# A two-layer hybrid state-space, attention and expert kernel: readout products reordered, mask added by VectorE in pieces, next layer's modulation products moved

## The chip, the core and the metric

The kernel runs on one core of one Trainium2 chip. The time is that of the device, in microseconds (us), from start to end of one execution, lower being better. A core has TensorE (matrix products; PE in the profile, PEld for its weight loads), VectorE (DVE), ScalarE (ACT), GpSimd (POOL) and SyncE (SP), each with a queue of its own that it works off in order. TensorE writes to PSUM, which has eight banks here: four take turns for products (`tile_ps`), two take transposes (`turn_ps`), two attention outputs (`out_ps`).

## What is computed

Two layers over 256 context and 256 latent tokens of width 1024, all in float32. A layer normalises its input, scales and shifts it by vectors made from a condition (the modulation), projects it once, and runs three mixers on the result. Then come a gated merge, an output projection and a mixture of 16 experts, two per token. The parts that the change touches, cut from the reference:

```python
sh1, sc1, g1, sh2, sc2, g2 = jnp.split((cond_lat @ w_mod[layer] + b_mod[layer])[:, None, :], 6, axis=-1)
...
# state space mixer: states are scanned both ways, then read out
y_lat = (readout(st_f[:, n_ctx:], 0) + readout(st_b[:, :n_lat], 1) + dsk * u_lat.astype(f32))
...
# grouped attention: query and key heads are normalised and rotated first
qa_h = rmsnorm(heads(qa, GQA_HEADS), q_norm_g)
...
# neighbourhood attention: scores get a bias table, and columns out of the window are masked
s_loc = jnp.einsum('bqhd,bikhd->bhqik', q_row, kb).astype(jnp.float32) * scale + bias[None]
s_loc = jnp.where(col_mask[None, None, :, None, :], s_loc, -jnp.inf)
```

## The kernel before

The order of work is written out by hand for each engine. `tile_jobs()` lists the jobs in TensorE's order; a job's place in the list, modulo 4, is its PSUM bank, and it may start when the job four places ahead has been taken out by ScalarE or VectorE. Weights stream through a ring of six 1 MB slots that SyncE refills as TensorE releases them, in the order of `slot_steps()`.

**Readout loop.** The 32 groups of state channels are read out in eight quarters of four groups, q = 0 to 7, with a ninth round for the last. For each q:

- GpSimd makes the coefficients `cp` of q in six operations (L1640 to L1645) in one of two buffers; it may start when the products `y` of q - 2 are complete.
- TensorE makes the lag products `z` of q (16 matrix products of 64 to 16, 32 records in the trace) from `cp`.
- ScalarE copies `z` out, VectorE adds the other half and the skip term (`readout_rows`), and ScalarE then issues eight DMAs (L1045) that spread it into the matrix `tm` of q. VectorE brings the carried states in (`carry_in`).
- TensorE makes `y` and `yb` of q (20 products, 40 records) from `tm`, `cp` and the states. They wait for the DMAs of `tm` (`tm_in`). ScalarE copies `y`, VectorE adds `yb` (L1479).

In round q the kernel before runs `z` of q first and `y` of q - 1 behind it. In the same round TensorE runs one part of the head norm (`qk_ms`, q up to 4), the modulation row product `mr` of block 4 + q (eight products over two ring slots), a projection (`in_loop`: two in round 0, one in each of rounds 1 to 4), the modulation columns `mc`, which wait for ScalarE's copy of the row (`mrow`), and the rotation `rope` (q up to 4). `rope` waits for `qnorm_done`: ScalarE takes a root, VectorE a reciprocal (L1486), and one more operation (L1487) scales the head. The root stands behind the eight DMA issues in ScalarE's queue. The `y` copy does too.

**Attention.** Layer 0 has 32 pairs of head and 128-query block, layer 1 has 16; half of them are grouped attention, the second half neighbourhood attention. In round n TensorE makes the scores of pair n, the transposes of pair n - 3 and the outputs of pair n - 4. VectorE takes maxima (L1514), reciprocals (L1520) and copies transposes (L1524); ScalarE takes exponentials (L1073); GpSimd scales the probabilities (L1660). In rounds 0 to 3 ScalarE also issues the four DMAs of the bias table (L972), in round 4 those of `yt` (L1085). GpSimd adds the mask of far columns to the table in two operations of 128x2048 ahead of pair 12 in layer 0 and pair 6 in layer 1 (L1654), once all four DMAs have landed (`bias_in`). In layer 0 the modulation blocks 0 to 3 of layer 1 (`mr`, ScalarE's copy, `mc`) stand in rounds 3, 7, 11 and 15.

## Time and profile before

| what | value |
|---|---|
| median of 3 runs | 2008.54 us (2006.32 to 2015.71) |
| the profiled execution | 2010.74 us, of it span 2009.1 us |
| TensorE busy | 1714.0 us (85%), mean granted clock 0.923 |
| VectorE, ScalarE, GpSimd busy | 637.3, 409.3, 347.9 us |
| readout loop, layer 0 and layer 1 | 209.9 to 336.2 us, 1307.4 to 1437.7 us |
| attention, layer 0 and layer 1 | 336.2 to 463.3 us, 1437.7 to 1508.9 us |

The span is from the first to the last instruction. A share of busy time is a mean over stages with different limits, so each stage is read by itself. The clock is what TensorE was granted: 1.0 is 2.4 GHz and 0.5 is 1.2 GHz, and a stretch's value is the mean of its parts at either. In the timeline a row joins instructions of one line that follow each other; the brackets say how long the engine had been idle and what released it. "ACTq" rows are DMA issues, during which ScalarE starts nothing else.

### The profile page before, as it was taken

How to read it: one execution, taken by the hardware profiler on the slowest of the kernel's cores; microseconds unless marked ns; L12 is line 12 of the kernel's file. 1: busy time of each engine (PE TensorE's matmuls, PEld its weight loads, DVE VectorE, ACT ScalarE, POOL GpSimd, SP SyncE). 2: the span in 40 equal slices, each digit the busy share in tenths (PEclk: the TensorE clock that was granted, in tenths of full speed). 3: DMA queues.
4: the chain of work that ended last, by engine and by line, in shares of the span. 5: the costliest groups of instructions: out<-in, count | busy, mean ns of one | idle time of the engine just before them, and what ended most of it. 6: DMA issues, size and time to landing. Idle time of an engine off the chain costs nothing.

```text
span 2009.1 us, 25439 instructions
## 1 busy us (share of the span) xinstructions
PE 1714.0 (85%) x9646; PEld 1049.6 (52%) x9646; DVE 637.3 (32%) x1378; ACT 409.3 (20%) x842; POOL 347.9 (17%) x284
## 2 busy tenths in 40 slices
PE   4999987899999998499979588998879994797794
PEld 1467554454444443355545336755458883464452
DVE  2578642351110113111101367774351112110012
ACT  3111211452000003122212231121242002121122
POOL 0004353681000000100000100435480000000000
PEclk8999986899999999699999788998789997899896
DMA  8411356508412125599999422145703427999992
GB/s 315 149 59 63 122 204 165 164 19 293 168 63 105 67 80 208 210 377 357 384 395 397 145 80 69 43 163 200 166 19 126 168 84 324 341 390 398 399 375 79
DMA packets 104882, 398.33 MB, mean 198 GB/s; under 512 B 43056, under 2 KB 52272, under 8 KB 64336
## 3 DMA queue, kind: packets, MB, share of 16 engines
q1 hardware_dynamic: 46960, 327.01, 41.9%
q10 hardware_dynamic: 50720, 29.54, 6.2%
q0 software_dynamic: 7104, 40.37, 5.9%
q8 instruction: 73, 1.20, 0.2%
q14 instruction: 25, 0.20, 0.0%
HBM read 370.67 MB, written 38.80 MB: 204 GB/s over the span
## 4 chain that ended last, share of the span: by engine, by line
PE 60%; DMA 14%; POOL 7%; DVE 6%; issue 5%; SPq 3%; ACT 3%; ACTq 1%; POOLq 0%; DVEq 0%
PE tile_ps L534 53%; DMA arena<-sorted_in 5%; PE turn_ps L534 4%; SPq L481 3%; DMA ring<-in_wpack 3%; POOL arena L1660 2%; DMA vn<-in_wpack 2%; DMA arena<-in_wpack 2%; PE out_ps L534 1%; DMA sorted_in<-arena,rows 1%; POOL arena L1654 1%; PE turn_ps L749 1%; ACTq L1045 1%; DVE rstd L1316 1%; POOL arena L1645 1%
## 5 line engine op out<-in xcount | busy, mean ns | idle before, releaser
L534 PE MATMUL tile_ps<-h,ring 128*128 128x512 f32 (+1 forms) x1312 | 475.3, 517 | 10.7 <-ACT h L930 8.0
L534 PEld LDWEIGHTS tile_ps<-h,ring 128*128 128x128 f32 x1312 | 250.6, 193 | 221.1 <-issue 206.0
L534 PE MATMUL tile_ps<-arena 64*16 64x128 f32 (+4 forms) x2032 | 244.2, 359 | 37.2 <-POOL arena L1645 16.5
L534 PE MATMUL tile_ps<-arena,ring 128*128 128x512 f32 (+1 forms) x704 | 235.3, 486 | 2.7 <-issue 2.7
L534 PEld LDWEIGHTS tile_ps<-arena 128*64 128x64 f32 (+3 forms) x2032 | 170.9, 161 | 94.1 <-issue 51.3
L534 PEld LDWEIGHTS tile_ps<-arena,ring 128*128 128x128 f32 x704 | 133.6, 190 | 96.6 <-issue 87.6
L1660 POOL TENSOR_SCALAR arena<-arena,smx 128x512 f32<-128x512 f32 (+1 forms) x96 | 127.9, 1349 | 86.8 <-DVE smx L1520 86.4
L534 PE MATMUL tile_ps<-ring,arena 128*64 128x256 f32 (+1 forms) x624 | 101.5, 469 | 9.9 <-ACT arena L1131 7.2
L1684 POOL DMA_DIRECT2D arena<-sorted_in x40 | 20.4, 511 | 515.7 <-PE tile_ps L834 515.7
L1112 ACT ACTIVATE arena<-tile_ps 128x512 f32<-128x512 f32 (+1 forms) x56 | 27.5, 491 | 347.4 <-PE tile_ps L534 347.4
L1581 DVE TENSOR_TENSOR arena<-tile_ps,arena 64x256 f32<-64x256 f32 x40 | 16.7, 417 | 228.2 <-ACT arena L1128 228.2
L1548 DVE TENSOR_TENSOR arena<-tile_ps,arena 128x512 f32<-128x512 f32 (+1 forms) x32 | 17.9, 558 | 212.1 <-PE tile_ps L534 212.1
L1640 POOL TENSOR_TENSOR arena<-arena 128x640 f32<-128x640 f32 x16 | 22.0, 1375 | 360.1 <-PE tile_ps L534 359.9
L1620 POOL TENSOR_SCALAR h<-h,amuls,mods 128x256 f32<-128x256 f32 x12 | 12.1, 1014 | 404.1 <-DVE h L1320 356.9
L834 PE MATMUL tile_ps<-con,arena 64*128 64x64 f32 x336 | 35.1, 227 | 50.4 <-DMA arena<-sorted_in 50.4
L1574 DVE COPY arena<-tile_ps 128x512 f32<-128x512 f32 x42 | 29.1, 692 | 146.9 <-PE tile_ps L834 146.9
L1073 ACT ACTIVATE arena<-tile_ps,smx 128x512 f32<-128x512 f32 (+1 forms) x96 | 58.7, 616 | 77.9 <-DVE smx L1514 68.1
L534 PEld LDWEIGHTS tile_ps<-ring,arena 128*64 128x64 f32 x624 | 51.3, 143 | 43.5 <-issue 34.0
L749 PE MATMUL turn_ps<-con,arena 128*128 128x128 f32 x320 | 51.8, 291 | 25.8 <-POOL arena L1660 9.3
L534 PE MATMUL tile_ps<-ring,h 128*128 128x256 f32 (+1 forms) x384 | 72.7, 352 | 0.0
L534 PE MATMUL turn_ps<-kn,arena 128*64 128x256 f32 x240 | 59.4, 398 | 11.6 <-DMA vn<-in_wpack 9.8
L534 PEld LDWEIGHTS tile_ps<-ring,h 128*128 128x128 f32 x384 | 64.6, 195 | 7.1
(258 smaller groups left out, 2157.2 us busy)
## 6 DMA issues: line engine op xcount, KB each, us to landing
ring<-in_wpack SPq DMA_DIRECT2D x176, 1024.0 KB, 7.9
arena<-in_wpack SPq DMA_DIRECT2D x64, 1024.0 KB, 28.8
h<-in_wpack SPq DMA_DIRECT2D x20, 1024.0 KB, 27.9
qa<-in_wpack SPq DMA_DIRECT2D x12, 1024.0 KB, 14.4
qn<-in_wpack SPq DMA_DIRECT2D x12, 1024.0 KB, 16.6
kn<-in_wpack SPq DMA_DIRECT2D x12, 1024.0 KB, 18.6
vn<-in_wpack SPq DMA_DIRECT2D x12, 1024.0 KB, 21.0
arena<-sorted_in POOLq DMA_DIRECT2D x42, 256.0 KB, 7.6
```

The lines of the kernel that those rows point to most:

```text
L481: sp.dma_start(dst, src).then_inc(arrived, 16)
L534: return nc.tensor.matmul(out, lhsT, rhs, start=start, stop=stop)
L749: ins = nc.tensor.transpose(turn_ps[:, half, t * P:(t + 1) * P], probs[:, N % (LAG + 1), half, t * P:(t + 1) * P], c("ident"))
L834: ins = nc.tensor.transpose(rows_bank[:, k * BS:(k + 1) * BS], hrow[:, k * P:(k + 1) * P], c("ident")[0:BS, 0:BS])
L1045: act.dma_start(tm[j * GRP:(j + 1) * GRP, q % 2], zs[:, :, a:a + P]).then_inc(tm_in, 16)
L1073: A(probs[:, N % (LAG + 1), half, 0:nk], bank((l, "sc", n, half))[:, 0:nk], ACT.Exp, bias=smx[:, 0, at:at + 1], accum_out=smx[:, 1, at:at ...
L1112: free(job, A(sig[:, n % 2, c0:], bank(job)[:, c0:], ACT.Sigmoid))
L1316: link(dve.reciprocal(rstd[:, c0:], rstd[:, c0:]))
L1574: CP(hsT.rearrange("p k n -> p (k n)"), rows_bank).then_inc(hsT_done[l], 1)
L1640: link(TT(o0, pv[0], cv[0], ALU.mult))
L1660: pool.tensor_scalar(v, v, smx[:, 2, at:at + 1], None, ALU.mult).then_inc(prob_done, 1)
L1684: pool.dma_start(hrow, sorted_in[bass.ds(r * BS, BS)]).then_inc(hrow_in[l], 16)
```

## The change

Four edits, in both layers except the last.

- In each round of the readout loop `y` and `yb` of q - 1 now come ahead of `z` of q, on TensorE, ScalarE and VectorE alike. ScalarE's `y` copy so comes ahead of the eight DMA issues.
- The projections in the loop stand in rounds 0 (two), 1, 2, 4 and 5 instead of 0 (two), 1, 2, 3 and 4.
- The mask is added by VectorE in eight pieces of 128x512, two at the end of each of four rounds that end just ahead of neighbourhood attention: rounds 12 to 15 in layer 0, 4 to 7 in layer 1. VectorE waits for `bias_in` at the first of them, and for each piece before it goes on. GpSimd's two operations and the semaphore `bias_done` go.
- In layer 0, the products `mr` of block 0 of layer 1 stand ahead of the last `y`; its columns and block 1 stand between the loop and attention, and blocks 2 and 3 stand in rounds 1 and 2 of attention.

```diff
@@ -108,7 +108,7 @@
 BRANCHES = (1, 2, 0)
-EVERY = 4
+EARLY = {1: 2, 2: 3}
 
...
@@ -128,7 +128,7 @@
 
-    return fill[IN_LOOP:IN_LOOP + 2] if q == 0 else fill[IN_LOOP + 1 + q:IN_LOOP + 2 + q]
+    return [fill[IN_LOOP + n] for n, at in enumerate((0, 0, 1, 2, 4, 5)) if at == q]
 
...
@@ -204,18 +204,19 @@
         for q in range(NQ + 1):
+            names += [(l + 1, "mr", 0)] if q == NQ and l + 1 < LAYERS else []
+            names += [(l, "y", q - 1), (l, "yb", q - 1)] if q else []
             names += [(l, "z", q, 0), (l, "z", q, 1)] if q < NQ else []
-            names += [(l, "y", q - 1), (l, "yb", q - 1)] if q else []
             names += [(l, "qk_ms", q)] if q <= KW else []
             names += [(l, "mr", MOD1 + q)] if q < NQ else []
             names += in_loop(fill, q)
             names += [(l, "mc", MOD1 + q)] if q < NQ else []
             names += [(l, "rope", q)] if q <= KW else []
+        names += [(l + 1, "mc", 0)] + mod_jobs(l + 1, [1]) if l + 1 < LAYERS else []
         n_pairs = len(attention_pairs(l))
         for u in range(n_pairs + LAG + 1):
             names += [(l, "sc", u, 0), (l, "sc", u, 1)] if u < n_pairs else []
-            if l + 1 < LAYERS and u % EVERY == EVERY - 1 and u // EVERY < MOD1:
-                names += mod_jobs(l + 1, [u // EVERY])
+            names += mod_jobs(l + 1, [EARLY[u]]) if l + 1 < LAYERS and u in EARLY else []
         for kind, *at in mix_order():
...
@@ -675,18 +676,8 @@
                 for q in range(NQ + 1):
-                    if q < NQ:
-                        pe.wait_ge(cp_done, l * NQ + q + 1)
...
-                                             cp[d, r, at_q, lags].rearrange("p a b -> p (a b)"), r == 0, r == 1)
-                                    if (g, r) == (GQ - 1, 1):
-                                        full((l, "z", q, n), ins)
+                    if q == NQ and l + 1 < LAYERS:
+                        modulation(l + 1, 0, l)
                     if q:
...
@@ -706,6 +697,18 @@
                         full(bwd, b)
+                    if q < NQ:
+                        pe.wait_ge(cp_done, l * NQ + q + 1)
+                        for n in range(2):
+                            wait_bank(pe, (l, "z", q, n))
...
+                                        full((l, "z", q, n), ins)
                     if q <= KW:
...
@@ -720,6 +723,10 @@
                         product((l, "rope", q), [(c("rot"), v)], bank((l, "rope", q))[:, 0:LAT])
+                if l + 1 < LAYERS:
+                    modulation_columns(l + 1, 0)
+                    modulation(l + 1, 1, l)
+                    modulation_columns(l + 1, 1)
 
...
@@ -736,9 +743,9 @@
                                                         qq[a:a + HD, q0:q0 + P], kk[a:a + HD, 0:nk]))
-                    early = l + 1 < LAYERS and n % EVERY == EVERY - 1 and n // EVERY < MOD1
+                    early = l + 1 < LAYERS and n in EARLY
                     if early:
-                        modulation(l + 1, n // EVERY, l)
+                        modulation(l + 1, EARLY[n], l)
                     if LAG <= n < len(us) + LAG:
...
@@ -1032,6 +1039,11 @@
 
+                    if q == NQ and l + 1 < LAYERS:
+                        copy_rows(l + 1, 0)
+                    if q:
+                        job = (l, "y", q - 1)
+                        copy(job, ug[:, (q - 1) * GQ:q * GQ].rearrange("p g c -> p (g c)"), bank(job)[:, 0:GQ * NCH])
                     if q < NQ:
...
@@ -1055,6 +1064,8 @@
 
+                if l + 1 < LAYERS:
+                    copy_rows(l + 1, 1)
                 for q in range(NQ):
...
@@ -1466,10 +1477,6 @@
                 for q in range(NQ + 1):
-                    if q < NQ:
-                        if q:
-                            readout_rows(l, q)
-                        carry_in(q)
                     if q:
...
@@ -1496,6 +1507,9 @@
                         TT(v[:, CTX:], v[:, CTX:], qrt[:], ALU.add).then_inc(rope_done, 1)
+                if l + 1 < LAYERS:
+                    for n in range(2):
+                        modulation_block(l + 1, n)
 
...
@@ -1523,8 +1536,15 @@
                             .then_inc(turn_free[0], 1)
-                    if l + 1 < LAYERS and n % EVERY == EVERY - 1 and n // EVERY < MOD1:
-                        modulation_block(l + 1, n // EVERY)
+                    if l + 1 < LAYERS and n in EARLY:
+                        modulation_block(l + 1, EARLY[n])
+                    part = n - len(us) // 2 + 4
+                    if 0 <= part < 4:
+                        dve.wait_ge(bias_in, 16 * GRID_H * (l + 1))
+                        for half in range(2):
+                            b = bias[:, part // 2, (part % 2 * 2 + half) * 2:(part % 2 * 2 + half + 1) * 2]
+                            b = b.rearrange("p h r c -> p (h r) c")
+                            link(TT(b, b, spread(c("far_cols"), 1, 2 * GRID_H), ALU.add))
 
...
@@ -1647,11 +1667,6 @@
                 for n in range(len(us)):
-                    if n == 3 * len(us) // 8:
-                        pool.wait_ge(bias_in, 16 * GRID_H * (l + 1))
-                        for qt in range(2):
-                            b = bias[:, qt].rearrange("p h r c -> p (h r) c")
-                            TT(b, b, spread(c("far_cols"), 1, HEADS * GRID_H), ALU.add).then_inc(bias_done, 1)
                     N, nk = n_before[l] + n, us[n][3]
```

In the rows of order below, of layer 0, `arena 16x128` are the `z` products, `arena 128x64` the `y` and `yb` products, `ring,csil` is `mr`, `con,mrow` is `mc`, `h,ring` a projection, `qa,con` is `rope`, and `ka,qa` are scores.

TensorE in the readout loop, from one `rope` to the next, before:

```order
L534 MATMUL tile_ps<-qa,con 128x256
L534 MATMUL tile_ps<-arena 16x128 x16
L534 MATMUL tile_ps<-arena 128x64 x20
L534 MATMUL tile_ps<-qsq,con 128x512
L534 MATMUL tile_ps<-ring,csil 32x512 x8
L534 MATMUL tile_ps<-h,ring 128x512 x8
L534 MATMUL tile_ps<-con,mrow 128x2 x4
L534 MATMUL tile_ps<-qa,con 128x256
```

And of the change, the same round:

```order
L535 MATMUL tile_ps<-qa,con 128x256
L535 MATMUL tile_ps<-arena 128x64 x20
L535 MATMUL tile_ps<-arena 16x128 x16
L535 MATMUL tile_ps<-qsq,con 128x512
L535 MATMUL tile_ps<-ring,csil 32x512 x8
L535 MATMUL tile_ps<-h,ring 128x512 x8
L535 MATMUL tile_ps<-con,mrow 128x2 x4
L535 MATMUL tile_ps<-qa,con 128x256
```

The `z` products have changed places with the `y` products; nothing else of the round has moved.

TensorE from the last `z` of layer 0 into attention, before:

```order
L534 MATMUL tile_ps<-arena 16x128 x16
L534 MATMUL tile_ps<-arena 128x64 x20
L534 MATMUL tile_ps<-ring,csil 32x512 x8
L534 MATMUL tile_ps<-con,mrow 128x2 x4
L534 MATMUL tile_ps<-arena 128x64 x20
L534 MATMUL tile_ps<-ka,qa 128x256 x4
L534 MATMUL tile_ps<-ka,qa 128x512 x4
L534 MATMUL tile_ps<-ring,csil 32x512 x8
L749 MATMUL turn_ps<-con,arena 128x128 x4
```

And of the change:

```order
L535 MATMUL tile_ps<-arena 16x128 x16
L535 MATMUL tile_ps<-ring,csil 32x512 x8
L535 MATMUL tile_ps<-con,mrow 128x2 x4
L535 MATMUL tile_ps<-ring,csil 32x512 x8
L535 MATMUL tile_ps<-arena 128x64 x20
L535 MATMUL tile_ps<-con,mrow 128x2 x4
L535 MATMUL tile_ps<-ring,csil 32x512 x8
L535 MATMUL tile_ps<-con,mrow 128x2 x4
L535 MATMUL tile_ps<-ka,qa 128x256 x4
L535 MATMUL tile_ps<-ring,csil 32x512 x8
L535 MATMUL tile_ps<-con,mrow 128x2 x4
L535 MATMUL tile_ps<-ka,qa 128x512 x2
```

One `mr` now stands ahead of the last `y`, one block between it and the first scores, and one behind the scores of pairs 0 and 1; a fourth follows behind those of pair 2.

VectorE in rounds 3 to 5 of the attention of layer 1, before (L1514 maxima, L1520 reciprocal, L1524 copy of a transpose):

```order
L1514 TENSOR_REDUCE smx<-tile_ps 128x1 x2
L1520 RECIPROCAL smx<-smx 128x2
L1524 COPY arena<-turn_ps 128x512
L1514 TENSOR_REDUCE smx<-tile_ps 128x1 x2
L1520 RECIPROCAL smx<-smx 128x2
L1524 COPY arena<-turn_ps 128x512
```

And of the change:

```order
L1527 TENSOR_REDUCE smx<-tile_ps 128x1 x2
L1533 RECIPROCAL smx<-smx 128x2
L1537 COPY arena<-turn_ps 128x512
L1547 TENSOR_TENSOR arena<-arena,con 128x512 x2
L1527 TENSOR_REDUCE smx<-tile_ps 128x1 x2
L1533 RECIPROCAL smx<-smx 128x2
L1537 COPY arena<-turn_ps 128x512
```

Two pieces of the mask stand between a round's copy and the next round's maxima.

## Rows read from the trace of the kernel before

**Rows 1.** The page, section 4: the chain that ended last, share of the span by engine.

```profile
PE 60%; DMA 14%; POOL 7%; DVE 6%; issue 5%; SPq 3%; ACT 3%; ACTq 1%; POOLq 0%; DVEq 0%
```

**Rows 2.** Busy time by stretch. Bounds in us: length, PE, PEld, DVE, ACT, POOL, clock, DMA.

```profile
209.88:336.16 126.28, 112.69 (x793) 68.55 (x794) 54.84 (x115) 16.50 (x32) 51.60 (x36) 0.85 0.42 148
336.16:463.27 127.11, 103.44 (x802) 60.76 (x803) 58.43 (x150) 59.48 (x173) 88.67 (x68) 0.90 0.40 108
1326.90:1437.73 110.83, 96.47 (x794) 65.48 (x794) 49.32 (x115) 14.80 (x32) 50.97 (x36) 0.86 0.49 169
```

**Rows 3.** Timeline, TensorE, readout loop of layer 0. Start us, length us, engine, work.

```profile
189.86 1.92 PE L534 MATMUL tile_ps<-arena 64*16 64x128 f32 x32
...
246.17 5.89 PE L534 MATMUL tile_ps<-arena 64*16 64x128 f32 x72
...
253.04 1.92 PE L534 MATMUL tile_ps<-ring,csil 128*32 128x512 f32 x16
...
255.43 7.11 PE L534 MATMUL tile_ps<-h,ring 128*128 128x512 f32 x16 [0.47 <-ACT arena L913]
...
263.19 0.68 PE L534 MATMUL tile_ps<-qa,con 128*128 128x256 f32 x2
```

**Rows 4.** Timeline, ScalarE's DMA issues and VectorE in that same iteration.

```profile
249.27 5.60 ACTq L1045 DMA_DIRECT2D arena<-arena  x8
...
255.91 3.35 DVE L1486 RECIPROCAL rstd<-rstd 128x512 f32<-128x512 f32 x1
...
259.30 0.75 DVE L1487 SCALAR_TENSOR_TENSOR qa<-qa,qg,rstd 128x512 f32<-128x512 f32 x1
```

**Rows 5.** Timeline, one iteration of the readout loop of layer 1.

```profile
1341.89 5.89 PE L534 MATMUL tile_ps<-arena 64*16 64x128 f32 x72 [0.86 <-POOL arena L1645]
...
1345.00 5.66 ACTq L1045 DMA_DIRECT2D arena<-arena  x8
...
1353.30 0.71 DVE L1487 SCALAR_TENSOR_TENSOR qa<-qa,qg,rstd 128x256 f32<-128x256 f32 x1
...
1356.87 5.99 PE L534 MATMUL tile_ps<-arena 64*16 64x128 f32 x72 [0.64 <-POOL arena L1645]
```

**Rows 6.** Timeline, the last iterations of the readout loop of layer 0.

```profile
296.01 10.27 PE L534 MATMUL tile_ps<-arena 64*16 64x128 f32 x72 [3.92 <-POOL arena L1645]
...
319.68 5.12 ACTq L1045 DMA_DIRECT2D arena<-arena  x8
...
329.65 6.71 PE L534 MATMUL tile_ps<-arena 128*128 128x64 f32 x40 [2.85 <-DMA arena<-arena]
```

**Rows 7.** Timeline, attention of layer 0: modulation columns after pairs 11 and 15, the mask.

```profile
385.85 1.05 PE L534 MATMUL tile_ps<-con,mrow 128*128 128x2 f32 x8 [0.95 <-ACT mrow L913]
...
392.58 9.01 POOL L1654 TENSOR_TENSOR arena<-arena,con 128x2048 f32<-128x2048 f32 x2
...
405.14 1.86 PE L534 MATMUL tile_ps<-con,mrow 128*128 128x2 f32 x8 [0.95 <-ACT mrow L913]
```

**Rows 8.** Timeline, attention of layer 1; second row: its bias DMA, us to landing.

```profile
1447.42 3.96 ACTq L972 DMA_DIRECT2D arena<-in_rpb  x1
...
arena<-in_rpb ACTq DMA_DIRECT2D x1, 512.0 KB, 11.0
...
1447.80 1.29 DVE L1514 TENSOR_REDUCE smx<-tile_ps 128x1 f32<-128x512 f32 x2 [1.11 <-PE tile_ps L534]
...
1449.08 0.67 DVE L1524 COPY arena<-turn_ps 128x512 f32<-128x512 f32 x1
...
1484.28 22.01 POOL L1660 TENSOR_SCALAR arena<-arena,smx 128x512 f32<-128x512 f32 x14 [2.11 <-DVE smx L1520]
```

**Rows 9.** VectorE beside GpSimd: two timeline rows, one group (busy us, mean ns, idle before).

```profile
223.24 1.54 POOL L1645 TENSOR_TENSOR arena<-arena 128x640 f32<-128x640 f32 x1
...
223.44 1.88 DVE L1487 SCALAR_TENSOR_TENSOR qa<-qa,qg,rstd 128x512 f32<-128x512 f32 x1
...
L1554 DVE TENSOR_TENSOR arena<-arena 128x512 f32<-128x512 f32 x16 | 11.1, 693 | 0.5
```

30 lines of the change are left out of this document (15 added, 15 removed).

## The prediction

> **What bounds the kernel now.** Read the chain of work that ended last first: TensorE holds 60% of it, DMA 14%, GpSimd 7% and VectorE 6% [rows 1]. TensorE is the bound of most stages but not of those that the change touches. The table by stretches shows these: in the readout loop of layer 0 TensorE is busy 112.7 of 126.3 us, in that of layer 1 96.5 of 110.8, in attention of layer 0 103.4 of 127.1, with a mean clock of 0.85 to 0.90 [rows 2]. So about 14, 14 and 24 us of idle time are there, and some time at the 1.2 GHz level. Then read one round of each loop for the wait that ends last.
>
> Layer 0, a round with a projection: `z` and `y` start at 246.17, take 5.89, and `rope` ends 0.6 us after 263.19, so a round is 17.6 us. The only wait in it is 0.47 us for ScalarE's `y` copy, which stands behind the DMA issues [rows 3, 4]. TensorE bounds this round. Layer 1: `z` starts at 1341.89 and again at 1356.87, 15.0 us, both times on GpSimd's coefficients [rows 5]. GpSimd starts them when `y` is complete, and `y` ends 5.9 us into the round, so about 9 us of coefficients and 5.9 us of products make up the round. GpSimd bounds it. Late rounds of layer 0 wait 3.92 us for GpSimd and 2.85 us for the DMAs of `tm`, and the same 72 records take 10.27 us instead of 5.89 [rows 6, 3]: 4.4 us to the clock's lower level after idle time.
>
> **Part 1, `y` ahead of `z`.** It removes the 0.47 us wait and, where GpSimd bounds, lets coefficients start earlier. But it closes two chains that were open. In the kernel before, `y` of q comes a whole round after `z` of q and with `z` of q + 1 between; now `y` of q is the next thing after `rope` of q. So from the end of `z`, two things must be over before the next `y`: head norm and `rope` (rounds up to 4), and the DMAs of `tm`.
>
> The head norm, layer 0: `z` is 1.85 us long (its row of 1.92 less the overlap) and ends at 248.0; the first DMA issue comes 1.25 us later, the eight take 5.60, the reciprocal starts 1.04 after them, and the scaling ends at 260.05, 12.05 after `z` [rows 3, 4]. The `y` copy leaves the queue ahead of the root, 0.25 less: 11.8. `rope` follows with 0.7: 12.5. TensorE's own work from `y`'s end at 252.06 to `rope`'s end at 263.8, without the wait, is 11.3, so the chain is late by 1.2. A round becomes 12.5 + 4.0 + 1.85 = 18.35 us, 0.75 more than 17.6. Four rounds: +3 us. Round 3 loses its projection of 7.1 us and gains nothing by it, since the chain is as long without.
>
> Layer 1: `z` ends at 1343.74, the scaling at 1354.01 [rows 5], so 10.3 - 0.25 + 0.7 = 10.7, and a round is 16.55 against 15.0: +1.55 in each of three. In round 4 the head is 512 wide, and its reciprocal is 3.35 us [rows 4], twice that of the 256 columns of the rounds before: +3.3. Together +8 us.
>
> Rounds 5 to 7 and the last `y` have no `rope`; there the DMAs bind. From `z`'s end: 1.25 to the first issue, 5.12 for eight, and in the one row where `y` waits it starts 4.85 after the last issue's end [rows 6]: 11.2 us. The lower bound is the issues alone, 6.4. That row has the ring's weight loads beside it, the other rounds don't wait and so show no landing; I take 8.5. The Trainium skill (DMA: Bandwidth & Descriptors, Anatomy of one DMA) gives a DMA some 2.0 us of fixed cost; by it the step would be nearer 8 and the sum 3 us less, and the row above, at 4.85, is beyond it. A round is then 8.5 + 5.85 = 14.35, and 15.75 for round 5 in layer 0, where 1.9 + 7.1 + 0.9 of TensorE's work are longer. Layer 0: 15.75 + 2 x 14.35 + 4.0 = 48.5 at full clock. Before it is a round of 15.0 and the 40.2 from 296.01 to the loop's end: 55.2, of which some 8 are the lower clock. TensorE still idles about 5.5 us in each of two rounds, so I leave 7.5 of these 8 in: 56.0, +0.8. Layer 1: 3 x 14.35 + 4.0 + 3 for the clock = 50.0 against 50.7: -0.6.
>
> **Part 2, projections and products moved.** The projection of round 5 and `mr` of block 0 stand in waits for `tm`; priced above or nothing, and if the DMAs land early, their 1.9 us come out. Between loop and attention stand the columns of block 0, `mr` of block 1, a copy of its row and its columns: 0.95 + 1.92 + 0.85 + 0.95 = 4.7 us [rows 3, 7], up to 7.5 at the lower clock; ScalarE's issues of the bias table wait behind them. I take 5. In attention, the blocks of rounds 7 and 11 go: each 1.92 of `mr`, 0.95 waiting for the row, 1.05 of columns, 3.9 us [rows 3, 7], of which GpSimd's pace leaves 3.3: -6.6. Blocks 2 and 3 come in rounds 1 and 2, one goes in round 3, where ScalarE's issues of the bias table stop it in any case; bounds -4 and +4, I take -1.5. A ring slot of `qn` is now held up to round 5; the two slots of modulation behind it are released one round later. The ring has six slots and a round without projection takes two, so three rounds' weights are in it: nothing.
>
> **Part 3, the mask.** GpSimd loses 9.01 us in each layer [rows 7]. In layer 1 it works without a gap in the second half, 14 operations in 22.01 us, 3.14 per pair [rows 8], so its loss would shorten the stage one to one. VectorE gains eight operations with both inputs in SBUF; the nearest such row is 0.69 us [rows 9]. Two prices come on top. First, a wait: the last bias DMA is issued at 1447.42 and lands 11.0 later, at 1458.4; VectorE is through with round 4's copy at 1449.75 [rows 8]. It stands there for 8.7 us, and the next maxima, on which exponentials, GpSimd and TensorE hang, stand behind it. ScalarE is then held by its own DMA issues, so of that only the two pieces count, 1.4 us. Second, a collision: at 223.44 a VectorE operation with two SBUF inputs took 1.88 us instead of 0.75; a GpSimd operation had begun at 223.24 and ended at 224.78, and 224.78 + 0.54 is where VectorE ends [rows 9, 4]. It ran behind GpSimd's. The pieces start 0.7 us after the reciprocal that starts GpSimd on a pair, and each waits for the one before. So in a round: 1.57 GpSimd, 0.69 piece, 1.57, 0.69, then maxima 1.29 and reciprocal 0.16, 6.0 us instead of 3.14. Three rounds: +8.6. Layer 1's attention: -9.0 + 8.6 + 1.4 = +1; without collision -9.0 + 1.5 + 1.4 = -6. I take -1, nearer to the row. The Trainium skill (SBUF — State Buffer, Who interferes with whom) says so too: a VectorE instruction with two SBUF inputs and a GpSimd one that reads SBUF exclude each other for whole instructions. This trace agrees, 1.88 against 0.75.
>
> Layer 0, rounds 12 to 15: from the columns of round 11 to those of round 15 are 19.3 us now, mask and one block in it [rows 7]. By the same sum with two narrow pairs it would be 20, without collision 11. I take 16.3: -3.
>
> **Sum.** Loops: layer 0 +3 + 0.8 + 5 = +8.8; layer 1 +8 - 0.6 = +7.4. Attention: layer 0 -6.6 - 1.5 - 3 = -11.1; layer 1 -1. Total +4.1 us. The profiled execution was 2010.7 us, 2.2 above the median of the runs, so 2014.8 there and 2013 as a median. A measurement of this kernel tells about 0.5%, 10 us, from no change: the forecast is no change.
>
> **Rivals.** *The idle time is filled and the clock stays up.* With rounds 5 to 7 fuller, TensorE keeps the upper level: -7.5 in layer 0, -3 in layer 1, and pieces that don't collide give -5 in each attention: about -16 after the sum's +4, 1992. For it speaks that the low clock comes after idle rounds [rows 6]; against it, that round 3 becomes an idle round, some 8 of 18 us, and the collision's row.
>
> *The DMA chain decides, slower.* `y` now waits for `tm` in six rounds, three in each layer, and each microsecond that the DMAs land later than 8.5 costs 6. At 9.5 the total passes +10; at 10.5, still under the row of 11.2 with weight loads in flight [rows 6], it is +16: 2025. For it: SyncE refills the ring in the same rounds, and late `y` brings low clock, 4.4 us at a time. Against it: the row may be the worst of eight.
>
> *The y copy's wait was all.* If `rope` doesn't bind because ScalarE's issues are shorter (5.12 in rows 6, not 5.60), loops cost 4 less; that stays inside the forecast.
>
> **Chances.** Forecast, within 0.5% of before: 0.42. First rival: 0.27, all faster. Second: 0.31, slower. The range takes in most of both, 1993 to 2026; the forecast's own is 2004 to 2018.
>
> **What would show it.** In the changed profile, `rope` in rounds 1 to 4 should wait for VectorE's scaling and a round be 18.4 (layer 0) and 16.5 us (layer 1); `y` of rounds 5 to 8 should wait for DMA; GpSimd should never be waited for in the loop. In attention a piece should take 1.5 us or more beside GpSimd's, and in layer 1 VectorE should stand about 8 us at its first piece. It is wrong if rounds stay at 17.6 and 15.0, or if pieces all take 0.7.

## The result and the profile after

The changed kernel takes 2102.85 us (median of 4 runs, 2097.05 to 2108.74), the kernel before beside it 2009.73 (4 runs, 2006.32 to 2015.71). The ratio is 1.046 with a 95% interval of 1.042 to 1.050: slower by 4.6%, far outside the predicted 1993 to 2026 us. The profiled execution took 2108.74 us, of it a span of 2107.0, against 2010.74 and 2009.1.

Where the 97.9 us of span are, by the stages of the timeline (z0 is the first `z`; a loop ends with its last `y`, an attention where the gates begin):

| us | before | after | difference |
|---|---|---|---|
| start to z0 of layer 0 | 189.9 | 195.7 | +5.8 |
| readout loop, layer 0 | 146.5 | 190.8 | +44.3 |
| attention, layer 0 | 127.0 | 125.5 | -1.5 |
| up to z0 of layer 1 | 844.0 | 841.2 | -2.8 |
| readout loop, layer 1 | 130.6 | 186.0 | +55.4 |
| attention, layer 1 | 71.0 | 67.1 | -3.9 |
| the rest | 500.1 | 500.7 | +0.6 |

The two readout loops hold all of it (+99.7; the other rows add up to -1.8). The row at the start is in stages that the change doesn't touch, and it comes and goes between kernels (z0 lay between 185.0 and 195.7 in all that were run).

The chain of work that ended last, from the page of the changed kernel, answers to [rows 1]:

```profile
PE 55%; DMA 17%; DVE 10%; issue 5%; SPq 4%; ACTq 3%; POOL 3%; ACT 2%; POOLq 0%; DVEq 0%
```

Of TensorE's 60% five points went to DMA (14 to 17) and VectorE (6 to 10); GpSimd, the releaser of the loop of layer 1 before, fell from 7% to 3%. The stretches of the changed kernel that answer to [rows 2], the loop of layer 0, that of layer 1 and the two attentions (in us: bounds, length, busy time of TensorE, its weight loads, VectorE, ScalarE, GpSimd, then granted clock, DMA share, GB/s):

```profile
216.45:386.45 170.00, 135.04 (x808) 85.38 (x808) 72.16 (x114) 17.55 (x33) 53.88 (x36) 0.72 0.37 123
1372.75:1539.25 166.50, 117.90 (x795) 84.46 (x795) 68.84 (x115) 14.66 (x32) 53.84 (x36) 0.70 0.34 113
386.45:512.02 125.57, 102.65 (x787) 59.35 (x785) 64.17 (x158) 58.78 (x172) 81.01 (x66) 0.88 0.37 93
1539.25:1606.30 67.05, 54.89 (x451) 34.01 (x449) 44.45 (x89) 35.42 (x89) 50.37 (x32) 0.93 0.39 64
```

Two things changed in the loops: TensorE idles 35 us in that of layer 0 instead of 14, and its clock fell from 0.85 and 0.86 to 0.72 and 0.70, so that the same products are busy longer. Adding up the timeline rows of the 544 records of `y` and `z` from the first pair on gives 53.6 us before and 72.8 after in layer 0, 51.2 and 71.7 in layer 1; adding up the idle times gives 13.5 and 35.6, 14.4 and 48.5.

TensorE's timeline of the changed kernel, two rounds of layer 0, with `rope` and without, to be laid beside [rows 3, 6]. The 72 records now are `y` and then `z`:

```profile
240.99 9.98 PE L535 MATMUL tile_ps<-arena 128*128 128x64 f32 x72 [2.73 <-DMA arena<-arena]
...
261.07 0.95 PE L535 MATMUL tile_ps<-con,mrow 128*128 128x2 f32 x8
262.53 0.70 PE L535 MATMUL tile_ps<-qa,con 128*128 128x256 f32 x2 [0.50 <-DVE qa L1498]
263.06 8.61 PE L535 MATMUL tile_ps<-arena 128*128 128x64 f32 x72
...
333.18 7.45 PE L535 MATMUL tile_ps<-arena 128*128 128x64 f32 x72
340.56 1.92 PE L535 MATMUL tile_ps<-ring,csil 128*32 128x512 f32 x16
347.95 1.87 PE L535 MATMUL tile_ps<-con,mrow 128*128 128x2 f32 x8 [5.47 <-ACT mrow L920]
357.03 10.24 PE L535 MATMUL tile_ps<-arena 128*128 128x64 f32 x72 [7.21 <-DMA arena<-arena]
```

The round from 240.99 takes 22.1 us, the one ahead of it (from 216.45) 24.5, where [rows 3] gave 17.6. The pair takes 7.4 to 10.2 us instead of 5.89, also where hardly any idle time is ahead of it. And `y` waits for a DMA. The second round in the other queues, ScalarE's issues of `tm` and SyncE's refills of the ring (the first start, length):

```profile
325.02 5.12 ACTq L1057 DMA_DIRECT2D arena<-arena  x8
...
341.78 2.40 SPq L482 DMA_DIRECT2D ring<-in_wpack  x4
341.97 5.25 ACTq L1057 DMA_DIRECT2D arena<-arena  x8
```

`z` ends at 340.6, `mr` starts there and releases ring slots, and SyncE sends for four slots of 1 MB from 341.78 on, while ScalarE issues the eight 32 KB DMAs of `tm` (341.97 to 347.22). `y` starts at 357.03, 9.8 us after the last issue. In the kernel before, `y` stood between `z` and `mr`: the issues began at 249.27 and `mr` at 253.04 [rows 3, 4], and SyncE's refills went out from 254.26 on, as the last of the eight was issued. The view of the line that issues them, in the changed kernel (landings count from the start of an issue):

```profile
who waited for it (us, times):
  PE tile_ps L535: 37.9, 10
...
DMA to landing us min/median/max: 2.0/6.6/11.0
```

Before, the same view said 2.0, 2.1 and 11.0, and TensorE waited once, 2.8 us [rows 6]. The Trainium skill (DMA: Bandwidth & Descriptors, Anatomy of one DMA) fits a fixed cost of about 2.0 us to DMAs that GpSimd issues; the shortest of these, which ScalarE issues, take the same 2.0. Of one that is under way together with refills that sentence gives no figure.

### The profile page after: what moved, and what is told of

Same layout as the page of the kernel before. It is cut to its first block, busy times and chain, and to the rows that moved or that the text cites. A ratio compares the mean times of both kernels' runs of the same rounds, so it can differ in the third digit from the quotient of the medians.

```text
span 2107.0 us, 25427 instructions
## 1 busy us (share of the span) xinstructions
PE 1760.7 (84%) x9646; PEld 1085.8 (52%) x9646; DVE 685.8 (33%) x1394; ACT 409.3 (19%) x842; POOL 337.3 (16%) x280
## 4 chain that ended last, share of the span: by engine, by line
PE 55%; DMA 17%; DVE 10%; issue 5%; SPq 4%; ACTq 3%; POOL 3%; ACT 2%; POOLq 0%; DVEq 0%
PE tile_ps L535 49%; DMA arena<-sorted_in 5%; DMA arena<-arena 4%; SPq L482 4%; PE turn_ps L535 4%; ACTq L1057 3%; POOL arena L1675 2%; DMA vn<-in_wpack 2%; DMA ring<-in_wpack 1%; DMA arena<-in_wpack 1%; DMA sorted_in<-arena,rows 1%; PE out_ps L535 1%; PE turn_ps L756 1%; DVE rstd L1327 1%; DVE x L1610 1%
## 5 line engine op out<-in xcount | busy, mean ns | idle before, releaser
L535 PE MATMUL tile_ps<-arena 64*16 64x128 f32 (+4 forms) x2032 | 284.2, 402 | 56.6 <-DMA arena<-arena 37.9
L535 PEld LDWEIGHTS tile_ps<-arena 128*64 128x64 f32 (+3 forms) x2032 | 202.1, 194 | 121.9 <-issue 87.1
L1675 POOL TENSOR_SCALAR arena<-arena,smx 128x512 f32<-128x512 f32 (+1 forms) x96 | 130.1, 1371 | 135.6 <-DVE smx L1533 135.2
L535 PE MATMUL tile_ps<-ring,arena 128*64 128x256 f32 (+1 forms) x624 | 100.5, 466 | 10.2 <-ACT arena L1142 7.2
L535 PE MATMUL tile_ps<-con,mrow 128*128 128x2 f32 x192 | 34.0, 299 | 58.2 <-ACT mrow L920 58.2
L535 PEld LDWEIGHTS tile_ps<-con,mrow 128*128 128x128 f32 x192 | 33.1, 257 | 78.8 <-ACT mrow L920 75.8
## 6 DMA issues: line engine op xcount, KB each, us to landing
qn<-in_wpack SPq DMA_DIRECT2D x12, 1024.0 KB, 16.8
```

The source lines that it names most:

```text
L535: return nc.tensor.matmul(out, lhsT, rhs, start=start, stop=stop)
L1675: pool.tensor_scalar(v, v, smx[:, 2, at:at + 1], None, ALU.mult).then_inc(prob_done, 1)
```

## Experiments

All ratios are to the kernel before, run beside each kernel on the same chip. Loop lengths are those of the profiled executions, as in the table above.

**The order of `y` and `z` alone, and the rest without it.** Edit of the first, on the kernel before (the same swap on ScalarE, VectorE and in the job list); the second is the changed kernel with this undone:

```diff
                 for q in range(NQ + 1):
-                    if q < NQ:
-                        ...z of q
                     if q:
                         ...y and yb of q - 1
+                    if q < NQ:
+                        ...z of q
```

> The kernel before with only the readout products y put ahead of the next readout product z (on TensorE, ScalarE, VectorE and in the order of PSUM banks); projections, modulation products and the mask stay as they were. Theory (landing): with y ahead, the ring slots that the modulation products release are refilled while the DMAs of tm are issued, so tm lands 6 to 11 us after its issue, y waits for it, and the products that follow the wait run at the lower clock. Then the order alone carries the whole loss and a little more: 2100 to 2120 us, both readout loops some 45 us and more longer, median landing of tm 6 us or more. Rival 1 (the other parts share it: products between loop and attention, projection of round 3 gone, the mask on VectorE): the order alone gives at most 60 us, 2040 to 2070. Rival 2 (collision of VectorE with GpSimd in the loop, VectorE's carry now beside the coefficients): as long as the theory says, but with tm landing in 2 to 3 us and TensorE waiting for VectorE.

> The changed kernel with only the order of y and z put back: projections in rounds 0, 0, 1, 2, 4, 5, modulation products at the loop's end and in rounds 1 and 2 of attention, and the mask on VectorE all stay. Theory (landing): the whole loss goes, and attention keeps what it gained: loops within 5 us of before, attention 10 us shorter in sum, 1995 to 2008 us. Rival 1 (the parts share the loss): 2040 us or more.

The order alone: 2115.69 us, ratio 1.053 (1.049 to 1.057), loops 193.9 and 190.7, so +47.4 and +60.1. Its landing of `tm` and who waited for it:

```profile
  PE tile_ps L534: 45.3, 11
...
DMA to landing us min/median/max: 2.0/6.4/12.8
```

With the order put back: 2006.65 us, ratio 0.999 (0.997 to 1.002), loops 144.7 and 136.6. Both rivals that shared the loss among the parts fall: the order carries all of it. The rival of the collision asked for a landing of 2 to 3 us, and it is 6.4. That says where, not yet by which mechanism.

**Refills held back.** The changed kernel, with the slots that a round's `mr` has used released at its columns:

```diff
-                        if k == 0:
+                        if k == 0 and l == during and n >= MOD1:
+                            held[n] = held.get(n, 0) + RELEASE[l].get((*job, half), 0)
+                        elif k == 0:
                             begin_job((*job, half), ins, during)
...
+                    if t == 0 and held.get(n):
+                        ins.then_inc(slot_used, held.pop(n))
```

> The changed kernel, but the two ring slots that a modulation product of the loop has used are released at that block's columns instead of at its first product, so that their refill starts after the DMAs of tm are issued. Nothing else is changed. Theory (landing): median landing of tm back at 2 to 3 us, y waits little, 38 us of waits and about as much again of lower clock go: 2020 to 2045 us. Rival (closed chain): the order itself makes a round as long as z, copy, issues, root, reciprocal and rope, the engine idles in it whatever the landing is, and the clock stays low: only the waits for DMA go, 2065 to 2080 us. Rival (the refill is late now): projections wait for their weights instead, 2100 us or more.

2061.61 us, ratio 1.027 (1.023 to 1.031): 41 us less than the changed kernel, loops 167.3 and 162.2 (-23.5 and -23.8). The landing, in this kernel:

```profile
DMA to landing us min/median/max: 2.0/2.0/6.0
```

No `y` waits for a DMA any more. So the refills beside the issues are the cause of the late landing, and holding them back is worth 47 us of the 100 in the two loops. But 2062 lies between the 2020 to 2045 of the theory and the 2065 to 2080 of the rival of the closed chain, nearer to the rival: the loops are still 20.8 and 31.6 us longer than before. Two things are left. The first is idle time. TensorE's, in both loops together, by what ended it:

| us | before | changed | refills held back |
|---|---|---|---|
| GpSimd's coefficients | 16.5 | 0 | 0 |
| the DMAs of `tm` | 2.9 | 37.9 | 0 |
| ScalarE's copy of the `mr` row, ahead of `mc` | 5.3 | 37.8 | 35.5 |
| VectorE's scaling, ahead of `rope` | 0.6 | 8.4 | 7.3 |
| other copies of ScalarE | 2.6 | 0 | 0 |

The row copy stands behind the eight issues. In the order before, `y` lay between `z` and `mr` and covered most of that; now `mr` follows `z` at once, and the columns wait. They start 7.1 to 7.5 us after the end of `z` in every round with neither projection nor `rope`, held back or not. A row of the kernel with refills held back (the profile gives "issue" as the releaser of most of these waits; ScalarE's copy of the row runs from 325.18 to 325.77):

```profile
325.87 1.84 PE L535 MATMUL tile_ps<-con,mrow 128*128 128x2 f32 x8 [5.66 <-issue]
327.57 10.24 PE L535 MATMUL tile_ps<-arena 128*128 128x64 f32 x72
```

The second is the clock. TensorE's, first in one of this kernel's pairs of `y` and `z`, which stood behind 0.40 us of idle time (the second number is the length, then busy time, clock, DMA share, GB/s):

```profile
230.07:232.00 1.93, 1.93 (x22) 1.00 0.87 352
232.00:234.00 2.00, 2.00 (x16) 0.60 1.03 434
234.00:236.00 2.00, 2.00 (x19) 0.50 0.59 250
236.00:238.50 2.50, 2.50 (x26) 0.50 0.03 7
```

and in a pair of the kernel before, which has `z` first:

```profile
228.56:230.50 1.94, 1.94 (x34) 1.00 0.00 0
230.50:232.50 2.00, 2.00 (x21) 1.00 0.00 0
232.50:234.40 1.90, 1.90 (x21) 1.00 0.27 52
```

With `y` first the clock falls to 1.2 GHz about two microseconds into the pair, though TensorE never stops. What it did before it fell is columns (2 wide), `rope`, and 64-wide products; in the kernel before, `z` (128 wide) stands between. The 544 records take 67.4 and 73.0 us in the two loops here; the pairs of 10.1 us and more among them stand behind idle time of 3 to 6 us, those of 7.4 to 8.6 behind half a microsecond at most. What stands ahead is not the whole cause. The first pair of layer 1, behind 14 us of projections, columns and `rope` and without a wait, kept the upper clock in the changed kernel and lost it in this one:

```profile
1372.75 5.79 PE L535 MATMUL tile_ps<-arena 128*128 128x64 f32 x72
...
1346.33 8.56 PE L535 MATMUL tile_ps<-arena 128*128 128x64 f32 x72
```

**Products ahead of `y`.** The same kernel, with four products of 512 columns ahead of every `y`:

```diff
+                        for k in range(4):
+                            mm(turn_ps[:, 0, 0:NTOK], c("ident"), h[:, k, :])
                         wait_bank(pe, fwd)
```

> The kernel with later refills (previous run, 2061.6 us), and ahead of every y four more products of 512 columns whose result nobody reads, 0.445 us each at the upper clock, 1.8 us a round, 29 us in 16 rounds. It tells what the lower clock costs by itself: in the previous run the pair of y and z (72 products) takes 8.5 us after the short products of 2 and 256 columns with almost no idle time before it (granted clock 1.0, then 0.6, then 0.5), in the kernel before, z first, 5.9 at clock 1.0. Theory (what TensorE does ahead of y sets the clock in it): pairs go to 5.9 to 7 us and the added 1.8 us a round is about paid back, 2045 to 2065 us. Rival (the clock falls in y whatever stands ahead, or the wait after it sets it): pairs stay at 8.5 to 10 us and the added products come on top, 2075 to 2090 us.

2089.34 us, ratio 1.039 (1.036 to 1.042). TensorE's timeline, one round of layer 0:

```profile
229.04 0.95 PE L535 MATMUL tile_ps<-con,mrow 128*128 128x2 f32 x8
232.12 0.70 PE L535 MATMUL tile_ps<-qa,con 128*128 128x256 f32 x2 [2.14 <-DVE qa L1509]
232.66 5.29 PE L535 MATMUL turn_ps<-h,con 128*128 128x512 f32 x8
237.79 5.78 PE L535 MATMUL tile_ps<-arena 128*128 128x64 f32 x72
```

The added products are twice what the expectation said, since a product of float32 is two records: 3.6 us at the upper clock and 5.3 behind a wait, 58 us in 16 rounds at the least, of which 28 show in the time. The pairs went to 5.8 us in every round, 44.4 us for the 544 records in each loop instead of 67.4 and 73.0. The time landed where the rival put it, but by the larger filling; the pairs decide, and they went as the theory said: work of 512 columns ahead of `y` keeps the clock up inside it, in all sixteen places. Filling doesn't pay, since the wait for VectorE (2.14) and the filling lie on the chain: the loops grew by 19.0 and 17.7 us although the pairs gave back 23.0 and 28.6.

**`mr` ahead of `y`.** The changed kernel; the row product of the round moves ahead of `y` on TensorE, its copy likewise on ScalarE:

```diff
+                    if q < NQ:
+                        modulation(l, MOD1 + q, l)
                     if q:
                         ...y and yb of q - 1, then z of q
-                    if q < NQ:
-                        modulation(l, MOD1 + q, l)
```

> The changed kernel with the loop's own modulation product of a round (mr, 512 columns, 1.9 us, releases two ring slots) put ahead of y instead of behind z, its row copy on ScalarE ahead of the y copy. Theory (landing, and clock by what stands ahead of y): the refills run beside y and not beside the issues of tm, tm lands in 2 to 3 us, y starts after products of 512 columns at the upper clock, and the columns no longer wait 5 us for the row copy behind the DMA issues: 2015 to 2040 us, less than with later refills alone (2062). Rival (closed chain): z, copy, issues, root, reciprocal, rope bound the round at 17 to 19 us in rounds 1 to 4 and idle time keeps the clock low: 2055 to 2070 us.

2094.21 us, ratio 1.040 (1.038 to 1.043): outside both expectations, a miss. `tm` lands in 3.2 us at the median, and yet the loops are 184.0 and 181.4. Two rows of TensorE's timeline of layer 0 show what took over:

```profile
265.45 0.95 PE L535 MATMUL tile_ps<-con,mrow 128*128 128x2 f32 x8
276.31 1.22 PE L535 MATMUL tile_ps<-qa,con 128*128 128x256 f32 x2 [9.91 <-DVE qa L1498]
```

`z` ended at 264.5, and `rope` starts 11.8 us later on VectorE's scaling. This is the closed chain of the prediction, 11.8 us to the scaling, now bare: every product that I moved ahead of `y` lengthens the round, because nothing but `qk_ms`, columns and a projection is left to hide the chain. And five `y` late in the loops wait 44.3 us for `tm` (19.1 for two in layer 0, 25.2 for three in layer 1). The reason is the theory's own: in the rounds without `rope` little but columns is left between `z` and the next `mr`, so its refills again go out during the issues. In layer 0 the issues run from 330.36 to 335.94 and SyncE's two refills start at 331.30; the sixteen DMAs of `tm` of the last two rounds land in 6.4 us at the median, the forty of the five rounds ahead in 2.1. So this edit did not part the landing from the chain, and tests neither by its total.

**`mr` between `z` and `y`, in the order of before.** It brings the refills beside the issues of `tm`, but leaves a round between `tm` and its `y`:

```diff
                     if q < NQ:
                         ...z of q
+                    if q < NQ:
+                        modulation(l, MOD1 + q, l)
                     if q:
                         ...y and yb of q - 1
```

> The kernel before (z ahead of y), with the round's modulation product put between z and y, so that its two ring slots are refilled while the DMAs of tm are issued, as in the changed kernel, but y of a round still has the whole next round's z ahead of it. Theory: a late landing costs only where y stands directly behind it: tm lands in 5 us or more at the median (2.1 before), only the last y of each loop can wait for it, and the time stays within 12 us of before, 2005 to 2022. Rival (the collision of transfers costs in either order, since the refills are slowed as well): 2035 us or more.

2035.69 us, ratio 1.011 (1.006 to 1.017). The line that issues `tm` in this kernel:

```profile
  PE tile_ps L534: 6.1, 2
...
DMA to landing us min/median/max: 2.0/6.4/14.0
```

The landing is as late as in the changed kernel, and TensorE waits for it only ahead of the last `y` of each loop, 6.1 us against 2.9 before, and once 1.8 us for a copy of ScalarE that the landing had held (1390.26). The time is outside the theory's 2005 to 2022 and where the rival had put it, by another cause: TensorE waits for no refill in either loop. `y` ends 1.9 us later in a round, and GpSimd's coefficients start at its end. In layer 1, where GpSimd bounds the round, three of its rounds take 16.8 to 16.9 us where 14.9 to 15.3 were usual. TensorE's wait for GpSimd, by the view of waits, is 13.5 us in the loop of layer 0 and 16.9 in that of layer 1, from 6.7 and 9.8 before, and the loops grew to 153.3 and 147.9, by 24 us together. Late landing by itself costs some 5 us of waits here; in the changed kernel, with `y` directly behind it, 35 more than before.

**The other parts, one by one.** On the kernel before: projections alone (`in_loop` as in the change), the next layer's modulation products alone (`EARLY` and the blocks at the loop's end), the mask alone, twice, and the mask with its pieces at rounds -1, 0, 2 and 3 from the middle instead of -4 to -1:

```diff
-                    part = n - len(us) // 2 + 4
-                    if 0 <= part < 4:
+                    places = (-1, 0, 2, 3)
+                    if n - len(us) // 2 in places:
```

> The kernel before with only the loop's projections moved: rounds 0, 0, 1, 2, 4, 5 instead of 0, 0, 1, 2, 3, 4. In the run with the order put back the loop of layer 1 was 6 us longer than before and that of layer 0 was 2 us shorter. Theory (the projection is missed in round 3 and fills idle time in round 5): layer 0 within 3 us, layer 1 +3 to +6, whose GpSimd and ScalarE chain gets no shorter by it: 2010 to 2018 us. Rival (no cost, the 6 us come from the products at the loop's end or from chance): 2005 to 2012 us.

> The kernel before with only the next layer's modulation products moved: block 0 ahead of the last y of the loop, block 1 behind the loop, blocks 2 and 3 in attention rounds 1 and 2. Only layer 0 has them. By the prediction's sum loop +5 and attention -8, so -3 (2008); by the difference of the earlier runs (order put back 2006.7, mask alone 2001.6, projections alone no change) +3 to +8: 2012 to 2020.

> The kernel before with only the mask moved from GpSimd to VectorE, in four pieces of two operations. By the prediction's sum -4 us (2006), by the changed kernel's trace, where layer 1's attention takes 64 us against 71, -7 to -10: 2000 us. If pieces and GpSimd's operations exclude each other as the prediction priced it, a piece takes 1.5 us or more and the time is 2006 to 2010; if VectorE's wait for the bias table decides, 2012 or more.

> The kernel before with only the mask on VectorE in four pieces, once more, beside the kernel with filled waits. First time: ratio 0.996, interval 0.9925 to 0.9995. If that was real, 0.993 to 0.998 again; if it was chance, 1.0.

> The kernel before with the mask on VectorE, and its four pieces put where their pairs need them: after the maxima of pairs -1, 0, 2 and 3 counted from the first pair of the second branch, instead of -4 to -1, the pieces for heads 0 to 3 first. With pieces at -4 to -1 (2001.6 us) VectorE stands 9 to 11 us in layer 1 for the DMA of the bias table. Theory (that wait is on the path): three rounds of 3.3 us later most of it is over, 5 to 9 us less, 1993 to 1998 us. Rival (the wait is hidden by ScalarE, which is held by its own issues of that table): 2000 to 2004 us.

| kernel | median us | ratio (95%) | loops | attentions |
|---|---|---|---|---|
| projections alone | 2016.36 | 0.999 (0.997 to 1.002) | 152.0, 137.7 | 128.7, 71.1 |
| modulation products alone | 2019.47 | 1.004 (1.001 to 1.007) | 148.6, 132.0 | 135.9, 70.0 |
| mask alone | 2001.60 | 0.996 (0.9925 to 0.9995) | 143.7, 132.2 | 122.4, 66.3 |
| mask alone, again | 2005.00 | 0.997 (0.994 to 0.999) | 143.3, 135.6 | 121.9, 66.8 |
| mask, later pieces | 2007.27 | 0.997 (0.995 to 0.999) | 148.6, 131.8 | 120.7, 68.8 |

A single profile moves a loop by some 5 us (the loop of layer 0 took 143.3 to 148.6 in the kernel before and the three with the mask alone, which don't touch it), so the loops of this table tell nothing below that. The kernel before ran at 2009.9 us beside the first "mask alone", at 2013.8 beside projections and later pieces, at 2011.2 beside the other two, so between the expectations, which are in us, the ratios decide. The projections cost nothing that can be measured. The mask gains 4 to 5 us in each attention, twice. Later pieces gain no more (0.997 against 0.996 and 0.997), as their rival said, though not in its 2000 to 2004 us. The modulation products lose 0.4% where the sum had a gain; by the profile the loss is in attention, +8.9. The parts don't add up: with mask and modulation products together, the changed kernel has -1.5 there. In the kernel with them alone, TensorE's timeline has this row after round 1:

```profile
352.79 1.87 PE L535 MATMUL tile_ps<-con,mrow 128*128 128x2 f32 x8 [10.04 <-ACT mrow L920]
```

and ScalarE's timeline these:

```profile
341.40 10.65 ACTq L979 DMA_DIRECT2D arena<-in_rpb  x1
...
352.15 0.58 ACT L920 COPY mrow<-tile_ps 128x512 f32<-128x512 f32 x1 [9.83 <-issue]
```

The row copy of block 2 stands behind the issue of a bias DMA that takes 10.65 us, beside the refills that the block itself has released. In the kernel before the one block in those rounds waited 6.2 us. Nor is ScalarE stopped at once by such an issue, as the text ahead of the prediction has it: within the first microsecond of this one it still starts three short instructions (341.67, 341.76, 342.12), and only then stands still. A few rounds on, a transpose waits for a copy of ScalarE that stands behind 9.5 us of `yt` issues, where the kernel before had waited 1.87 us (its row starts at 364.45):

```profile
378.11 1.11 PE L756 MATMUL turn_ps<-con,arena 128*128 128x128 f32 x4 [7.18 <-ACT arena L1089]
```

From the loop's end to this row, where blocks 1 to 3 and the columns of block 0 now stand instead of block 0 alone, it is 43.7 us instead of 28.1; from it to the first scores of neighbourhood attention, now without the blocks of rounds 7, 11 and 15, it is 36.6 instead of 44.4.

**A version that beats both?** The mask alone, with four products of 512 columns ahead of `z` in rounds 6 and 7:

```diff
+                    if q in (6, 7):
+                        ...
+                        for k in range(4):
+                            mm(turn_ps[:, 0, 0:NTOK], c("ident"), h[:, k, :])
                     if q < NQ:
                         pe.wait_ge(cp_done, l * NQ + q + 1)
```

> The kernel before with the mask on VectorE in four pieces, and in rounds 6 and 7 of each readout loop four products of 512 columns ahead of z, whose result nobody reads. TensorE stands 4.3 to 4.7 us there for GpSimd's coefficients and then takes 7.9 us for z and y at the lower clock instead of 5.9. Theory (what TensorE does before the pair sets its clock): the products lie in the wait, pairs take 5.9 us, GpSimd starts the next coefficients 2 us sooner, four times: 8 to 12 us less than the same kernel without them. Rival: the products start late and run at the lower clock, 5.3 us or more, and push z back: no gain or a loss of up to 4 us.

1997.99 us, ratio 0.993 (0.990 to 0.996). It is faster than the kernel before and than the changed one. That the products add to the mask's gain isn't shown: the median is 7.0 us below that of the mask alone beside it, less than the 8 to 12 of the theory, the intervals of the two overlap (0.990 to 0.996, 0.994 to 0.999), and in the profiles the loops are 145.9 and 136.5 against 143.3 and 135.6, so the difference doesn't lie where the products stand. A round of it, TensorE's timeline:

```profile
300.81 1.05 PE L534 MATMUL tile_ps<-con,mrow 128*128 128x2 f32 x8 [1.45 <-ACT mrow L919]
301.72 5.38 PE L534 MATMUL turn_ps<-h,con 128*128 128x512 f32 x8
307.03 5.89 PE L534 MATMUL tile_ps<-arena 64*16 64x128 f32 x72
...
321.94 5.89 PE L534 MATMUL tile_ps<-arena 64*16 64x128 f32 x72 [0.17 <-POOL arena L1657]
```

The pair is back at 5.89 and the next one starts 14.9 us later, where the two kernels with the mask alone took 16.9 and 16.3; that much of the theory is seen. But the products took 5.38 where the wait had been 4.68, and the last `y` of the loops then waits 2.7 and 4.4 us for `tm`.

## Why the prediction was wrong, point by point

**The step that failed** is "Rounds 5 to 7 and the last `y` have no `rope`; there the DMAs bind. [...] the other rounds don't wait and so show no landing; I take 8.5." Three things in it were wrong, by size:

- *The landing.* 8.5 us from `z`'s end to `y` leaves 2.1 between the end of the last issue and `y`. Measured was 16.5 in the round shown (340.6 to 357.03), with 9.8 from the last issue on, beyond the upper bound of 11.2 too, and 16.6 in the same round of layer 1. In the four other places without `rope` the step took 9.1 to 12.5. The step took the durations of the issues from before and didn't ask what else the move starts: `mr` behind `z` releases two slots, so the swap moves the refills by the length of `y` into the issues. Holding the refills back gave 47 us in the two loops. The view of before, with a median of 2.1, had 11.0 as its longest, and the row of 4.85 had refills beside it, as the prediction says.
- *The rounds.* The DMAs were priced in the rounds without `rope` alone. In the changed kernel `y` waited for them in ten of sixteen places, seven of them with `rope` just ahead (in layer 0 0.67, 2.73, 4.29 and 2.46 us of wait, on top of a chain of 12). And "two things must be over before the next `y`" left out a third, the row copy and the columns behind it: with the refills held back, where no DMA is waited for, rounds without `rope` and projection still take 8.8 to 9.2 us from `z` to `y`, more than 8.5. TensorE's wait for the row copy, 37.8 us in the two loops of the changed kernel, has no term in the sum, though part of it lies inside the time that the DMAs would take anyway.
- *The clock.* The pair was put at 5.85 us everywhere, and the lower clock only where idle time was before. In the changed kernel it takes 7.4 to 10.2 in all rounds but one (5.79 at 1372.75), and by itself adds 19.2 and 20.5 us (72.8 - 53.6, 71.7 - 51.2). Even without late DMAs it adds 13.8 and 21.8 (67.4 and 73.0 with refills held back), part of it behind the waits for the row copy. That short products ahead of `y` bring the clock down, at no idle time to speak of, no row of before had shown.

**The second rival had the mechanism**, with "each microsecond that the DMAs land later than 8.5 costs 6" and 2025 us at 10.5. It had the size wrong as well: the step came 8 us later than 8.5 in two of its six places and 0.6 to 4.0 in the other four, 25 us in all, so its own rule gives some 2038 with the sum's +4. The rest is in the rounds with `rope`, which it left out, and in the clock, 40 us, of which it speaks only as 4.4 us at a time.

**The closed chain of the head norm was right.** For layer 0, 11.8 us to the scaling was predicted; from `z`'s end to the start of `rope` it is 11.5 to 11.6 in the changed kernel and with refills held back, and 11.8 in two rounds with `mr` ahead of `y`. In layer 1 10.05 was predicted and 9.7 measured. With refills held back a round of layer 0 is 20.5 and 20.6 us (209.53, 230.07, 250.69) against the predicted 18.35; with 8.5 for the pair in place of 5.85 the prediction gives 21.0.

**A collision that was not priced.** Since GpSimd starts at `y`'s end, its coefficients now run beside `carry_in`. VectorE and GpSimd in the changed kernel:

```profile
227.09 1.87 POOL L1663 TENSOR_TENSOR arena<-arena 128x640 f32<-128x640 f32 x1
...
227.79 1.42 DVE L1316 TENSOR_TENSOR arena<-arena 128x224 f32<-128x224 f32 x1
...
230.69 1.91 DVE L1314 TENSOR_TENSOR arena<-arena 128x224 f32<-128x224 f32 x2
...
233.06 0.39 DVE L1317 TENSOR_TENSOR arena<-arena 128x224 f32<-128x224 f32 x1
```

An operation of two SBUF inputs takes 1.42 us beside GpSimd's and 0.39 alone, so `carry_in` takes 6.4 us instead of the 3.1 of a round before. I had costed it at nothing, and in this round it is worth next to nothing:

```profile
232.42 0.69 ACT L930 ACTIVATE rstd<-tile_ps,con 128x512 f32<-128x512 f32 x1 [5.76 <-issue]
...
233.37 3.34 DVE L1497 RECIPROCAL rstd<-rstd 128x512 f32<-128x512 f32 x1
```

The reciprocal needs ScalarE's root, which ends at 233.11; it starts 0.26 us later.

**Attention.** Predicted for layer 0 were -11.1, and +5 for the blocks between, so -6; measured -1.5, the mask's -4.6 to -5.1 and a loss by the modulation products. The modulation products alone were -3 by the sum (+5 - 6.6 - 1.5) and +8.9 by the profile. The gain behind the issues is there (44.4 to 36.6 us, with a third block gone from it); what failed is "bounds -4 and +4" for blocks 2 and 3, which missed ScalarE's copies behind 10.65 and 9.5 us of issue. Layer 1 was put at -1 and measured -3.9, and -4.2 to -4.7 with the mask alone: the collision of pieces with GpSimd, +8.6 in the sum, didn't come. Both engines in layer 1's attention, changed kernel:

```profile
1560.30 1.42 DVE L1547 TENSOR_TENSOR arena<-arena,con 128x512 f32<-128x512 f32 x2 [9.46 <-DMA arena<-in_rpb]
...
1563.20 6.83 POOL L1675 TENSOR_SCALAR arena<-arena,smx 128x512 f32<-128x512 f32 x4 [6.95 <-DVE smx L1533]
1563.61 1.55 DVE L1547 TENSOR_TENSOR arena<-arena,con 128x512 f32<-128x512 f32 x2
```

Two operations take 1.55 us in the middle of GpSimd's work and 1.42 without it; GpSimd's take 1.71 each instead of 1.57 [rows 8]. The row that I had argued from [rows 9] is of a GpSimd operation with two tensors, this one has one. VectorE's stand at the first piece, predicted as 8.7, is 9.46.

**Its signs.** `rope` waiting for VectorE in rounds 1 to 4: seen in six of eight, but short (0.50 to 2.9 us). `y` of rounds 5 to 8 waiting for DMA: seen in five of eight, and in five of the eight earlier ones too. GpSimd never waited for in the loop: true in both. Rounds of 18.4 and 16.5: 19.5 to 25.6 in layer 0, 19.3 to 27.1 in layer 1. A piece of 1.5 us or more: not seen, the sixteen took 0.68 to 1.08.

**Open.** What brings the clock down inside `y` was tried only by filling, and the pair at 1372.75 is not explained. Of the 20.8 and 31.6 us that remain with refills held back, pairs are 13.8 and 21.8; the rest, 7.0 and 9.8, is idle time (18.1 for 13.5 and 24.7 for 14.4) and in layer 0 the product of block 0, 3.6. All this carries an uncertainty of some 5 us a loop. How much of the pairs' share would go with the waits for the row copy was not tried.

## What to carry to other kernels

When a step moves ahead of another, list what each of its neighbours releases, since transfers that were spread by the old order may now start together; and price a transfer that becomes the last thing waited for by the longest landing in its view, not by the median of a time when nobody waited. A consumer directly behind a chain of copy, issues and landing needs other work between, and the order before had exactly that: a whole round. Look also for a second consumer in the same queue: here a short copy behind the issues stopped TensorE for as long as the landing did (37.8 and 37.9 us). Work that holds only short products ahead of another stretch of short products can lose TensorE's upper clock without a wait, so look at the clock of the stretch, not only at idle time.

## What the runs showed of the hardware

- Eight DMAs of 32 KB within SBUF landed 2.0 us after their issue when alone, 6.4 to 6.6 at the median and up to 14.0 beside refills of 1 MB each, and back at 2.0 when the refills were held until after the issues.
- TensorE's clock fell from 2.4 to 1.2 GHz (1.00, 0.60, 0.50) within a busy pair behind 2-wide and 64-wide products, and stayed up (5.8 us instead of 8.5) behind eight records of 512 columns. One pair without them stayed up too (5.79 us).
- A VectorE operation with two SBUF inputs took 1.42 us instead of 0.39 beside GpSimd's operations of two tensors, and 0.78 instead of 0.71 beside those of one tensor and a scalar. The Trainium skill (SBUF — State Buffer, Who interferes with whom) has the two engines exclude each other for whole instructions when VectorE reads two inputs from SBUF and GpSimd reads SBUF; the first case agrees, the second doesn't.
- The issue of one bias DMA by ScalarE took 10.65 us beside refills of the ring. ScalarE started three short instructions within its first microsecond and then nothing for 9.83.
